# A hybrid decoder block on one core: the per-layer input is transposed by VectorE in 32x32 blocks instead of by TensorE

## The reference

```
h = rmsnorm(x, g_mix);  z = h @ w_in            # 1536 columns: a, b (512 each), v (512)
u = a * sigmoid(b)
u = causal_depthwise_conv(u, width 31) + conv_b
u = silu(layernorm(u, ln_g, ln_b))
q = multiscale_pool(v)                          # trailing means over 2/4/8/16, per-group 128x128 map, scale
x = x + concat(u, q) @ w_out
x = x + swiglu_ffn(rmsnorm(x, g_ffn))
gate = sigmoid(rmsnorm(x, g_ple_gate) @ w_ple_gate)
e = rmsnorm(p @ w_ple_up, g_ple_post)           # what the change is about: p @ w_ple_up
x = x + gate * e
out = rmsnorm(x, g_final)
```

## Time and profile before

| what | value |
|---|---|
| time, median of 3 runs (lowest to highest) | 1003.5 us (1003.3 to 1003.97) |
| the profiled execution: span, first to last instruction | 1001.1 us |
| the profiled execution: own time | not given beside its span; the span is 2.4 us under the median of the runs |
| TensorE matmuls busy | 990.6 us, 99% |
| TensorE weight loads busy | 822.1 us, 82% |
| VectorE, ScalarE, GpSimd busy | 750.3, 464.0, 385.3 us |
| mean granted clock of TensorE | 0.999 |
| the 16 transposes of p on TensorE, mean of one | 272 ns (they overlap) |
| share of TensorE in the chain that ended last | 95% |

### The profile page before, as it was taken

The page is one execution under the profiler, slowest core; times in us unless marked ns, Lnnn a source line. Parts: engine busy times, 40 slices in busy tenths (PEclk is TensorE's granted clock), DMA queues, the critical chain, the costliest instruction groups (busy, mean ns, idle before and its releaser), DMA issues.

```text
span 1001.1 us, 12499 instructions
## 1 busy us (share of the span) xinstructions
PE 990.6 (99%) x4543; PEld 822.1 (82%) x4543; DVE 750.3 (75%) x1017; ACT 464.0 (46%) x713; POOL 385.3 (38%) x288
## 2 busy tenths in 40 slices
PE   9999999999999999999999999999999999999996
PEld 7888888888888888888888888888888888888885
DVE  6899999956699575665665665763687888985887
ACT  7635348414363423333333333333444665675775
POOL 3446797710146444444354354451000000011745
PEclk9999999999999999999999999999999999999999
DMA  7421202551224233333332332413998788533222
GB/s 255 152 71 43 85 1 120 205 178 64 105 64 132 80 105 111 100 106 95 116 105 83 127 105 70 141 64 107 359 388 301 232 310 261 196 106 105 85 84 105
DMA packets 103518, 138.25 MB, mean 138 GB/s; under 512 B 6122, under 2 KB 60930, under 8 KB 103458
## 3 DMA queue, kind: packets, MB, share of 16 engines
q1 hardware_dynamic: 103312, 137.20, 40.8%
q10 hardware_dynamic: 146, 0.27, 0.1%
HBM read 104.68 MB, written 32.77 MB: 137 GB/s over the span
## 4 chain that ended last, share of the span: by engine, by line
PE 95%; DVE 2%; issue 1%; ACT 1%; POOL 1%; DMA 0%; POOLq 0%; ACTq 0%; DVEq 0%
PE ps L1552 31%; PE ps L1554 31%; PE ps L1553 31%; PE ps L1606 2%; DVE ftmp L2414 0%; DVE resid L2417 0%; DMA resid<-in_x 0%; DVE spare L1958 0%; ACT junk L975 0%; PE ps L1700 0%; PE ps L1710 0%; ACT act_hi L961 0%; POOL rs L705 0%; PE ps L1690 0%; POOL ss L702 0%
## 5 line engine op out<-in xcount | busy, mean ns | idle before, releaser
L702 POOL TENSOR_SCALAR ss<-ss 128x1 f32<-128x1 f32 x38 | 16.8, 441 | 320.1 <-ACT junk L975 298.8
L2049 DVE SCALAR_TENSOR_TENSOR ps<-resid,convw,ps 128x512 f32<-128x512 f32 x190 | 127.4, 750 | 0.0
L1552 PE MATMUL ps<-ring_hi,ring_lo 128*128 128x512 f32 x308 | 120.0, 390 | 0.1
L1554 PE MATMUL ps<-ring_hi 128*128 128x512 f32 x308 | 119.8, 389 | 0.0
L1553 PE MATMUL ps<-ring_lo,ring_hi 128*128 128x512 f32 x308 | 119.8, 389 | 0.0
L1552 PE MATMUL ps<-act_hi,bs_lo 128*128 128x512 f32 x240 | 93.6, 390 | 0.0
L1554 PE MATMUL ps<-act_hi,bs_hi 128*128 128x512 f32 x240 | 93.4, 389 | 0.0
L1553 PE MATMUL ps<-act_lo,bs_hi 128*128 128x512 f32 x240 | 93.4, 389 | 0.0
L961 ACT ACTIVATE ring_hi<-raw 128x512 fp32r<-128x512 f32 x89 | 51.9, 625 | 60.4 <-PE ps L1554 60.3
L708 POOL TENSOR_TENSOR wc_lo<-raw_b,wc_hi 128x1024 fp32r<-128x1024 f32 x22 | 58.4, 2656 | 48.7 <-ACT wc_hi L961 47.6
L1958 DVE TENSOR_TENSOR ring_lo<-raw,ring_hi 128x512 fp32r<-128x512 f32 x89 | 58.0, 688 | 22.9 <-ACT ring_hi L961 22.7
(11 more groups left out here) (279 smaller groups left out, 2713.7 us busy)
## 6 DMA issues: line engine op xcount, KB each, us to landing
raw<-in_w_gate_up SPq DMA_DIRECT2D x44, 512.0 KB, 5.2
raw<-in_scratch SPq DMA_DIRECT2D x52, 256.0 KB, 3.3
raw<-in_w_down SPq DMA_DIRECT2D x52, 256.0 KB, 4.1
in_scratch<-in_s SPq DMA_DIRECT2D x44, 256.0 KB, 2.7
in_scratch<-gtmp SPq DMA_DIRECT2D x33, 256.0 KB, 2.3
keep<-in_w_down SPq DMA_DIRECT2D x32, 256.0 KB, 4.6
keep<-in_scratch SPq DMA_DIRECT2D x25, 256.0 KB, 3.5
resid<-in_x SPq DMA_DIRECT2D x8, 512.0 KB, 7.0
```

Source lines behind the costliest of these rows:

```text
L702: pool.tensor_scalar(ss[:, n:n + 1], ss[:, n:n + 1], 1.0 / D, EPS, ALU.mult, ALU.add)\
L1552: pe.matmul(dst, w_lo_, m_hi, start=start, stop=False, skip_group_check=onto)
L1554: return pe.matmul(dst, w_hi_, m_hi, start=False, stop=stop, skip_group_check=onto)
L2049: dve.scalar_tensor_tensor(out=conv_c if k == last_odd else acc, in0=u_all[:, c, k + h * BANK:k + (h + 1) * BANK], scalar=convw[:, c * 32 ...
```

## The change

The load of p is split into eight DMAs, each for 32 partitions. A run is now 32 elements (128 bytes) long, and the 32x32 blocks are put down at the places that they have in the transposed matrix, so that only the inside of each block is still to be transposed. VectorE does that with two instructions of 128x1024 (`turn_p`), which write to `wide`; they stand behind steps 8 and 16 of unit 1 of the convolution. TensorE's 16 transposes and its waits for them are gone. ScalarE makes one copy of each half instead of two (`copy_p`), from `wide`, and the two halves have a place each, so that `copy_p(1)` doesn't wait for `p_low(0)`. The load of w_ple_up waits for `p_turned` as before, which VectorE now signals. The side jobs of units 4 to 7 are put behind other steps of the convolution.

```
-    p_v = p[0, 0].rearrange("(t p) d -> p t d", p=P)
+    p_v = p[0, 0].rearrange("(b j) d -> j b d", j=SQ)
...
-            sp.dma_start(raw_b[:, :, :].rearrange("p a (t d) -> p (a t) d", d=DP), p_v).then_inc(rawb_in, DMA)
+            for k in range(KP):
+                for a in range(P // SQ):
+                    first = k * P + a * SQ
+                    sp.dma_start(raw_b[a * SQ:(a + 1) * SQ, k, :].rearrange("j (b i) -> j b i", i=SQ),
+                                 p_v[:, :, first:first + SQ]).then_inc(p_in, DMA)
...
             def p_low(k):
-                pool.wait_ge(p_copied, 2 * (k + 1))
-                lo(bs_lo[:, k, :], wide[:, 1, HEADPAD:], bs_hi[:, k, :], p_lo_ok)
+                pool.wait_ge(p_copied, k + 1)
+                lo(bs_lo[:, k, :], wide[:, 1 + k, HEADPAD:], bs_hi[:, k, :], p_lo_ok)
...
                 act.wait_ge(p_turned, k + 1)
-                if k:
-                    act.wait_ge(p_lo_ok, k)
-                act.activation(wide[:, 1, HEADPAD:], pair(6), ACT.Copy).then_inc(p_copied, 1)
-                copy(bs_hi[:, k, :], pair(6), p_copied)
+                copy(bs_hi[:, k, :], wide[:, 1 + k, HEADPAD:], p_copied)
...
-                if n in (4, 5):
-
-                    k = n - 4
-                    if k:
-                        pe.wait_ge(p_copied, 2)
-                    else:
-                        pe.wait_ge(rawb_in, 2 * DMA)
-                    for h in range(HALVES):
-                        for q in range(HT):
-                            ins = pe.transpose(ps[:, 6 + h, q * P:(q + 1) * P],
-                                               raw_b[:, :, :].rearrange("p a (t d) -> p (a t) d", d=DP)
-                                               [:, h * HT + q, k * P:(k + 1) * P], ident[:, :])
-                    ins.then_inc(p_turned, 1)
...
                     pe.wait_ge(taps_done, TAPS_0)
-                    pe.wait_ge(p_copied, 2 * KP)
...
-            for j in range(KC):
-                convolve(j, {})
-            convolve(4, {13: lambda: ln_stats(range(0, 2)), 19: lambda: ln_scale(range(0, 2)),
-                         25: lambda: ln_stats(range(2, 4))})
-            convolve(5, {3: lambda: ln_scale(range(2, 4)), 23: silu_0})
-            convolve(6, {2: mix_low_0, 9: silu_2, 11: mix_low_2, 17: lambda: q_low(0), 21: lambda: q_low(1),
-                         25: lambda: q_low(2)})
-            convolve(7, {3: lambda: q_low(3)})
+            def turn_p(k):
+                dve.wait_ge(p_in, KP * (P // SQ) * DMA)
+                dve.wait_ge(tables_ok, N_TABLES)
+                dve.transpose(wide[:, 1 + k, HEADPAD:], raw_b[:, k, :]).then_inc(p_turned, 1)
+
+            convolve(0, {})
+            convolve(1, {8: lambda: turn_p(0), 16: lambda: turn_p(1)})
+            convolve(2, {})
+            convolve(3, {})
+            convolve(4, {7: lambda: ln_stats(range(0, 2)), 13: lambda: ln_scale(range(0, 2)),
+                         18: lambda: ln_stats(range(2, 4))})
+            convolve(5, {1: lambda: ln_scale(range(2, 4)), 14: silu_0, 19: mix_low_0})
+            convolve(6, {2: silu_2, 4: mix_low_2, 9: lambda: q_low(0), 13: lambda: q_low(1),
+                         17: lambda: q_low(2), 21: lambda: q_low(3)})
+            convolve(7, {})
```

More of the change, by code:

```diff
@@ L35 @@
 HEADPAD = 16
+SQ = 32
 DMA = 16
@@ L210, in hybrid_block @@
         pw_lo_ok = sem("pw_lo_ok")
+        p_in = sem("p_in")
         p_turned = sem("p_turned")
@@ L1065, in _ @@
             copy_p(1)
-            act.wait_ge(rawb_in, 3 * DMA)
+            act.wait_ge(rawb_in, 2 * DMA)
             for r in range(KP):
```

## The result

The changed kernel takes 1006.14 us (median of 9 runs, 1005.74 to 1006.59), the kernel before 1003.50 in the same series (9 runs, 1003.14 to 1004.74). The ratio is 1.0023, with a 95% interval of 1.0014 to 1.0032: 2.6 us slower, against a forecast of 1005.8. One execution each of e4, e9 and e11 was disturbed (1222 to 2595 us): no ratio has it in, the medians printed do (0.13 us at most), and as it was the profiled one of e9, that kernel's rows are read from a repeat, e11_gpsimd_again.

A forecast was written before the change was run, and what follows sets the result against it. TensorE, never waiting from 25 to 993 us, was taken as the bound: -1.74 removed, +0.45 at normed_turn, +2.6, +0.5 and +0.5 at q_group(0) to (2) make +2.3, so 1005.8 us, range 1002.6 to 1009.0.

The forecast's parts named there:

- transposes off TensorE: Sixteen transposes leave TensorE, in two groups of eight at 0.87 us each: 1.74 us saved.
- unit 5 starts: VectorE starts unit 5 at 136.5 instead of 133.88, 2.6 us late, even if the transposes cost nothing.
- wait at silu_0: VectorE waits 3.6 and 0.7 us at silu_0 for ScalarE's scale_shift pair.
- normed_turn(0, 2): TensorE wants the first mix_low at 157.15 for this turn and loses about 0.45 us.
- wait at q_group(0): TensorE waits 2.6 us at q_group(0), because VectorE's mix_low(3) ends only at 169.1.
- q_group(1) and (2): TensorE loses 0.5 us more at each of these q groups, which wait for q_low(0) and q_low(1).
- VectorE ends unit 7: At about 211 us, some 7.5 later than before, hidden from TensorE with 5 to 6 us of cover.
- a fall of the clock: Rival: TensorE's waits of up to 2.6 us cost some 2 us more in clock (1008); chance 0.04.
- the near one of its two ends: One VectorE transpose taken as 1.25 us, near a plain operation's 1.22; the far end was 2.78, two passes.
- early end of its 42 to 59 us: The short-run load of p lands between 42 and 59 us, hidden, as VectorE wants it at 64.1.
- The first check: At the v stage GpSimd's split is ready at 105.0, TensorE wants it at 105.4: it fits by 0.4 us.
- the rival on the other side: The new order works if silu_0's second y comes by 149.9, leaving only the 1.74 gain: 1001.8 us; chance 0.13.

The follow-up runs named there:

- e4: Changed kernel with the side jobs of units 4 to 7 at steps between the old and new places: 1002.62 us, ratio 0.9992 to the kernel before.
- e9: Changed kernel with unit_begun(5) moved behind window(1) in GpSimd's queue, from ahead of pooled_low(0): 1003.71 us, ratio 1.0001 to the kernel before.
- e11: The same kernel as e9 run once more, for the profile of an undisturbed execution: 1003.62 us, ratio 0.9998 to the kernel before.
- e5: Changed kernel with the second VectorE transpose cut from 1024 to 32 columns (product half wrong): 1006.25 us, ratio 1.0032 to the kernel before.
- e2: Changed kernel with the side jobs of units 4 to 7 back at their old steps: 1006.90 us, ratio 1.0031 to the kernel before.
- e3: Kernel before with only the side jobs of units 4 to 7 at their new steps: 1007.98 us, ratio 1.0047 to the kernel before.
- e6: Changed kernel with each of VectorE's two transposes done twice, output the same: 1009.64 us, ratio 1.0067 to the kernel before.
- e1: Changed kernel with scale_shift(0) and (1) put ahead of pooled_high(1) in ScalarE's queue: 1002.80 us, ratio 0.9992 to the kernel before.
- e8: The order of e4 with q_low(3) moved from step 3 of unit 7 to step 24 of unit 6: 1001.86 us, ratio 0.9986 to the kernel before.

## Why the prediction was right

Its parts, by its own steps:

| step | forecast, us | measured, us |
|---|---|---|
| transposes off TensorE | -1.74 | -1.78 (98.87 to 97.09 from the early matmul to conv_turn(0)) |
| one transpose on VectorE | 1.25 | 1.23 and 1.24 |
| VectorE idle ahead of ln_stats(2..3) | 0.5 | 0.20 |
| unit 5 starts | 136.5 | 136.67 |
| pooled_low(0) starts | 138.0 | 138.17 |
| scale_shift(0) starts | 150.0 | 150.14 |
| wait at silu_0 | 3.6 and 0.7 | 3.48 and 0.64 |
| normed_turn(0, 2) | +0.45 | +0.26 |
| wait at q_group(0) | +2.6 | +2.82 |
| q_group(1) and (2) | +1.0 | +1.51 (e5, at the upper clock: +1.08) |
| VectorE ends unit 7 | 211 | 213.9 |
| conv_turn(4) | 217.0 | 217.70 |

The additions of TensorE are differences of starts: normed_turn(0, 2) is 157.55 - 116.46 = 41.09 behind conv_turn(0), for 40.83 before; q_group(0) 11.87 behind that, for 9.05; q_group(2) 9.93 further, for 8.42; conv_turn(4) 38.35 further, for 38.38. They sum to the 4.56 of the stretch.

What was off. The last term: I priced the waits at q_group(1) and (2) and gave a fall of the clock 0.04. It fell, and made that term 1.5 instead of 1.0; where it stayed up, in e5, the term is 1.08 and the loss in the stretch 4.15 for a forecast of 0.45 + 2.6 + 1.0 = 4.05. It fell behind four of the six waits of 1.86 us and more in these runs (the changed kernel, e2, e3, the first of e6), not in e5 nor in the second of e6; 0.04 was far too low a chance, and 2 us on top too high a price at this place, though not at those of e2 and e6 (1.7). The transpose came out at the near one of its two ends. The load landed just ahead of the early end of its 42 to 59 us. VectorE ended unit 7 at 213.9 and not 211. Of these 2.9 us 2.1 are unit 7's first two steps, which took 3.56 us beside GpSimd and not 1.42 (last section); the cover was 3.8 us and not 5 to 6, so it stayed hidden. The 2.4 added to the span for the runs holds the 0.4 of the fast profiled execution; as the forecast is a difference, nothing hangs on it.

The first check, 0.4 us of spare at the v stage, was confirmed by e6: 2.5 us more on VectorE gave a wait of 2.17 at that very stage. "Transposes that cost nothing at all would give the same 136.5" was confirmed by e5 for one of the two. The decisive point of the rival on the other side, that silu(1) must be free by 149.9, was named rightly as a matter of GpSimd's and ScalarE's queues: e1 moved it there and won 3.3 us. In the changed kernel nothing does so, and silu(1) began at 152.91.

What stays open: why the clock falls behind one wait of 2.41 us and not behind another, and the last 0.23 us between e8's 1.51 and the 1.74, which is inside what the measurement can tell.

## What to carry to other kernels

Taking work off the bounding engine wins only as long as those who feed it keep their phase. Here VectorE ran 2.4 us later and TensorE 1.7 earlier, so the side jobs had to move by about 4 us; silu_0, on which the loss hangs, was moved by nine steps (5.9 us), and a job placed ahead of its input stops the whole queue behind it. Before moving a job forward, follow its input back through every in-order queue to see whether it hangs on the very engine that is being rearranged: here VectorE waited for ScalarE, which waited for GpSimd, which waited for VectorE.

Keep guards such as unit_begun until it is known what they guard. Ahead of pooled_low(0) and window(1) this one frees no buffer that they use: they touch neither gain nor the sums of unit 5, and sum_taps(6), which changes gain, waits for ScalarE's first taps, which wait for the same step of unit 5. What it kept here was the length of two VectorE instructions.

## What the runs showed of the hardware

**Blocks transposed on VectorE cost as much as a plain operation.** 128x1024 of f32 in 32x32 blocks took 1.23 and 1.24 us, as a subtraction of the shape (1.22); the second of the two, at 70.91, had GpSimd at work beside it (69.68 to 72.09). The Trainium skill (VectorE: DVE Perf Modes, "The three transpose paths") has 311 ns for a 128x128 bf16 tile; eight of them would be 2.5 us, twice what was measured, so that figure doesn't scale to a wide tile.

**VectorE waits inside an instruction for GpSimd.** In the changed kernel the 190 steps with their sum in PSUM take 715 to 751 ns, whatever GpSimd does. Those with both tiles in SBUF take about 0.76 us with GpSimd idle, and up to 2.90 beside it. The changed kernel's unit 7, VectorE and then GpSimd:

```profile
191.82 3.56 DVE L2037 SCALAR_TENSOR_TENSOR ps<-resid,convw,gain 128x512 f32<-128x512 f32 x2
```

```profile
191.95 2.88 POOL L714 TENSOR_TENSOR bs_lo<-raw,bs_hi 128x1024 fp32r<-128x1024 f32 x1 [2.15 <-ACT bs_hi L967]
```

No wait is shown for it anywhere: it hides in the duration. The Trainium skill (SBUF — State Buffer, "SBUF: two separate sides") states it as an exclusive lock that a VectorE operation with two SBUF inputs and a GpSimd operation that reads SBUF take in turn, for a whole instruction. The trace agrees: the long step ends 0.56 us behind the end of GpSimd's instruction both here (195.39 and 194.83) and in e11 (140.75 and 140.19), and GpSimd's next one is late in turn (4.64 us for two in e11, 3.87 for such a pair at 153.93 in the changed kernel).

**The clock can fall behind short waits.** Between 25 and 993 us, after waits of TensorE of 1.86 to 2.42 us, the matmuls were 0.43 apart instead of 0.23 for some 3 us, in four cases of six: from about 1 us behind the wait in the changed kernel, at once in e6_transposes_twice (108.25). Waits of 0.85 us and less never did it.

It is no fixed property of a kernel either, by the mean clock of each execution: of the nine of the changed kernel five have 0.996 (median 1006.22 us) and four 0.998 (median 1006.04), where the kernel before has 0.997 to 0.999. In e2_order_before two executions took 1005.43 and 1005.49, on the forecast of 1005.4 that left the clock out, and four 1006.82 to 1007.44. One execution of each was profiled, so that the clock makes these differences is likely and not shown.

**Short runs cost little each, and move at less than half the rate.** In the microsecond from 38 on (row above) all the packets were runs of 128 B: at 161 GB/s one took an engine 128 x 16 / 161 = 13 ns, against 47 ns for 1 KB and 28 ns for 512 B before; the forecast had 14 on the line through both. Over the whole load the rate was 136 to 188 GB/s by the microsecond, with one of 25, for 348 of the 1 KB runs. The Trainium skill (DMA: Bandwidth & Descriptors, Specifications) speaks of a read-modify-write under 512 B; no run here can show that mechanism, and its price, if it is one, was covered. What did grow is the issue: eight such transfers held SyncE's queue for 12.35 us, one of 1 KB runs for 1.13.
